# Constants, first loads and the first norm in one stage, and the rotary tables moved into the cross attention's dense stage

## The reference

```python
# first block
x = x + parallel_mixer(rms_norm(x, g_mix), w_in, conv_w, ..., w_out)       # 1024 -> 3088 columns, then mLSTM and gMLP
x = x + memory_cross_attention(rms_norm(x, g_xattn), rms_norm(mem, g_mem), w_q_x, w_kv_x, w_o_x)
x = x + hier_moe(rms_norm(x, g_moe), ...)
x = rms_norm(x, g_final)
# second block, two layers
for l in range(2):
    mix = token_mixer(x, positions, ...)       # four branches; one of them (_mla) rotates by positions
    x = layernorm(alpha * x + mix, ...)
    x = layernorm(alpha * x + hier_moe2(x, ...), ...)

def rms_norm(x, g):
    return x * rsqrt(mean(x * x, axis=-1) + 1e-6) * g

def _rope(x, positions):                       # half = 16
    inv = 10000.0 ** (-arange(half) / half)
    ang = positions[..., None] * inv
    cos, sin = cos(ang), sin(ang)
    ...
```

## Time and profile before

| | |
|---|---|
| median of 3 runs | 3036.12 us (3034.94 to 3040.34) |
| the profiled execution, whole | 3035.32 us |
| its span, first to last instruction | 3033.6 us |
| TensorE busy | 2463.5 us, 81% of the span |
| VectorE, ScalarE, GpSimd busy | 1301.4, 889.5, 407.8 us |
| mean granted TensorE clock | 0.900 of full |

### The profile page before, as it was taken

One profiled execution on the slowest core, in us unless ns is written; L12 is line 12 of the kernel. 1 busy time (PEld: TensorE's weight loads), 2 busy tenths in 40 slices (PEclk: granted clock), 3 DMA queues, 4 the chain that ended last, 5 costly groups with the idle time before them and its releaser, 6 DMA issues. The chain is left out here.

```text
span 3033.6 us, 50648 instructions
## 1 busy us (share of the span) xinstructions
PE 2463.5 (81%) x18120; PEld 1934.1 (64%) x18121; DVE 1301.4 (43%) x2776; ACT 889.5 (29%) x1677; POOL 407.8 (13%) x718
## 2 busy tenths in 40 slices
PE   4975799888888886869899869983959989869882
PEld 4963788854444446757677857763848667757661
DVE  4437345521111115634753544335644754453334
ACT  2233234211111113144532313322233633213221
POOL 1000000022122210000000134442000000024333
PEclk9988899889999998979999869996979999969996
DMA  3200242679999954022121479993212212459993
GB/s 127 85 1 1 70 139 58 278 319 403 411 410 404 395 219 152 29 70 61 44 62 52 155 291 345 381 363 137 70 35 70 61 51 63 164 197 374 383 388 140
DMA packets 209305, 565.80 MB, mean 187 GB/s; under 512 B 26598, under 2 KB 170598, under 8 KB 184592
## 3 DMA queue, kind: packets, MB, share of 16 engines
q1 hardware_dynamic: 191104, 538.73, 47.8%
q0 software_dynamic: 18064, 25.23, 2.5%
HBM read 560.46 MB, written 36.18 MB: 197 GB/s over the span
## 5 line engine op out<-in xcount | busy, mean ns | idle before, releaser
L1027 PE MATMUL ps<-m_gate_up,e_xT 128*64 128x256 f32 x1088 | 271.4, 413 | 64.1 <-DMA m_gate_up<-in_w_gate_up 57.9
L1027 PEld LDWEIGHTS ps<-r_gate_up,e_xT 128*64 128x64 f32 x2272 | 264.3, 143 | 91.3 <-issue 87.7
L1027 PE MATMUL ps<-r_gate_up,e_xT 128*64 128x128 f32 x2272 | 276.8, 283 | 41.4 <-DMA r_gate_up<-in_w_exp_gate_up 34.2
L1029 PE MATMUL ps<-r_gate_up,e_xT 128*64 128x128 f32 x2272 | 276.9, 283 | 0.0
L1027 PEld LDWEIGHTS ps<-m_gate_up,e_xT 128*64 128x64 f32 x1088 | 160.6, 150 | 177.0 <-issue 113.3
L1181 DVE TENSOR_TENSOR e_hid<-e_silu,ps 64x128 f32<-64x128 f32 (+1 forms) x210 | 70.2, 335 | 473.3 <-ACT e_silu L1069 469.3
L1029 PE MATMUL ps<-m_gate_up,e_xT 128*64 128x256 f32 x1088 | 271.5, 413 | 0.0
L1029 PEld LDWEIGHTS ps<-r_gate_up,e_xT 128*64 128x64 f32 x2272 | 264.3, 143 | 0.0
L1069 ACT ACTIVATE e_silu<-ps 64x128 f32<-64x128 f32 (+1 forms) x210 | 63.6, 303 | 654.7 <-PE ps L1029 654.7
L2195 PE MATMUL ps<-t_hT,t0a_t0g_w 128*128 128x512 f32 x768 | 199.4, 411 | 4.6 <-DVE t0a_t0g_w L2217 2.4
L2195 PE MATMUL ps<-t_hT,t1a_t1g_w 128*128 128x512 f32 x768 | 198.1, 409 | 4.6 <-DVE t1a_t1g_w L2217 2.4
(11 more groups left out here) (647 smaller groups left out, 4793.9 us busy)
## 6 DMA issues: line engine op xcount, KB each, us to landing
m_gate_up<-in_w_gate_up SPq DMA_DIRECT2D x32, 4096.0 KB, 39.0
r_gate_up<-in_w_exp_gate_up SPq DMA_DIRECT2D x64, 2048.0 KB, 31.1
m_down<-in_w_down SPq DMA_DIRECT2D x32, 2048.0 KB, 38.9
r_down<-in_w_exp_down SPq DMA_DIRECT2D x64, 1024.0 KB, 34.0
t0a_t0g_raw<-in_w_in SPq DMA_DIRECT2D x32, 512.0 KB, 3.8
t1a_t1g_raw<-in_w_in SPq DMA_DIRECT2D x32, 512.0 KB, 3.8
mixw_raw<-in_w_in SPq DMA_DIRECT2D x10, 1024.0 KB, 5.2
xaw_raw<-in_w_kv_x SPq DMA_DIRECT2D x8, 1024.0 KB, 5.4
```

The lines of the kernel that those rows point to most:

```text
L1027: nc.tensor.matmul(ps_gu[q][0:SLOTS], xT[:, c, :], ring.gu[s][:, 0, c, span], start=c == 0, stop=c == DC - 1)
L1029: last = nc.tensor.matmul(ps_gu[q][SLOTS:P], xT[:, c, :], ring.gu[s][:, 1, c, span], start=c == 0, stop=c == DC - 1)
```

## The change

The constants, the load, the gate columns, `mask_ge` and the first norm become one stage, `start_up`. Its four engine blocks run side by side:

- SyncE issues x in four transfers, one for each tile, each with its own semaphore, then the columns, then nine transfers in a list, of which four are small rows, one the positions and four the mixer's constants. It waits for the list at the end.
- GpSimd makes all constants, `mask_ge` with them.
- VectorE computes, for each tile as it lands, statistics with `bn_stats` and `bn_aggr`, and from them mean square plus epsilon; the factor of a tile (`reciprocal`) comes behind the statistics of the next one. At the end it makes the gate columns.
- ScalarE takes a root of a value set to one before anything else, then for each tile the root and the scaling of the tile into the mixer's `y`.

The rotary tables become a class `Rope`. The angle chain runs on VectorE as the `side` of the cross attention's `dense` after chunk 0, and the two sines run on ScalarE, by a new argument `act_side`, after its items of chunk 1. `dense` gets two more arguments, `pe_side` and `banks`, which no call in the program sets.

```diff
-def dense(nc, name, k, chunks, items, raw_ring=3, side=None, before=None):
+def dense(nc, name, k, chunks, items, raw_ring=3, side=None, before=None, act_side=None, pe_side=None, banks=8):
...
                             act.wait_ge(bank_full, i + 1)
-                            it.out(nc.scalar, ps[0:it.rows, i % 8, 0:it.n]).then_inc(emptied["act"], 1)
+                            it.out(nc.scalar, ps[0:it.rows, i % banks, 0:it.n]).then_inc(emptied["act"], 1)
+                    if act_side is not None:
+                        act_side(act, c)
...
+def make_constants(nc, k, pool, made):
...
+    for n in ("ident", "mask_le", "mask_lt", "mask_ge"):
+        g.memset(k[n][:], 0.0)
...
+    g.affine_select(k["mask_ge"][:], k["mask_ge"][:], [[1, n]], ALU.is_ge, -BIG, P - S, -1)
...
+def start_up(nc, k, x, rows_of_x, h, columns, column_rows, loads, col):
...
+            @block.sync
+            def _(sp):
+                for t in range(TT):
+                    sp.dma_start(x[:, t, :], rows_of_x[t * P:(t + 1) * P]).then_inc(x_landed[t], 16)
+                sp.dma_start(columns[:], column_rows).then_inc(columns_landed, 16)
+                for dst, src in loads:
+                    sp.dma_start(dst, src).then_inc(late_landed, 16)
+                sp.wait_ge(late_landed, 16 * len(loads))
+
+            @block.gpsimd
+            def _(pool):
+                make_constants(nc, k, pool, made)
+
+            @block.vector
+            def _(dve):
+                link = Chain(dve, chain)
+                vec.memset(r[:, 4, :], 1.0).then_inc(cleared, 1)
+
+                def squares(t):
+                    at = slice(t, t + 1)
+                    dve.wait_ge(x_landed[t], 16)
+                    for q in range(D // 256):
+                        last = vec.bn_stats(stats[:, t, q, :], x[:, t, q * 256:(q + 1) * 256])
+                    link(last)
+                    link(vec.bn_aggr(mv[:, t, :], stats[:, t]))
+                    link(vec.scalar_tensor_tensor(r[:, 3, at], mv[:, t, 0:1], mv[:, t, 0:1], mv[:, t, 1:2], ALU.mult, ALU.add))
+                    vec.tensor_scalar(r[:, 0, at], r[:, 3, at], 1e-6, None, ALU.add).then_inc(mean_ready, 1)
+
+                def factor(t):
+                    dve.wait_ge(root_ready, t + 1)
+                    vec.reciprocal(r[:, 2, t:t + 1], r[:, 1, t:t + 1]).then_inc(factors_ready, 1)
+
+                for t in range(TT):
+                    squares(t)
+                    if t:
+                        factor(t - 1)
+                factor(TT - 1)
+                dve.wait_ge(columns_landed, 16)
+                for l in range(2):
+                    for n, w, f in (("half_b_gate", 32, 0.5), ("minus_b_gate", DC, -1.0)):
+                        vec.tensor_scalar(k[n][:, l * w:(l + 1) * w], col(f"b_gate{l}")[:, 0:w], f, None, ALU.mult)
+
+            @block.scalar
+            def _(act):
+                act.wait_ge(cleared, 1)
+                sca.activation(r[:, 4, 0:1], r[:, 4, 1:2], ACT.Sqrt)
+                for t in range(TT):
+                    act.wait_ge(mean_ready, t + 1)
+                    sca.activation(r[:, 1, t:t + 1], r[:, 0, t:t + 1], ACT.Sqrt).then_inc(root_ready, 1)
+                    act.wait_ge(factors_ready, t + 1)
+                    sca.activation(h[:, t, :], x[:, t, :], ACT.Identity, scale=r[:, 2, t:t + 1])
...
-            rms_rows(nc, "mixn", [(lambda t: x[:, t, :], lambda t: y[:, t, :], TT, D)], 1e-6, k["mixer_loads"])
+            k["start_up"](y)
...
-            dense(nc, "xaw", k, chunks, items,
+            rope = Rope(nc, sb, k)
+            dense(nc, "xaw", k, chunks, items, side=lambda dve, c, emptied: rope.angles(dve) if c == 0 else None,
+                  act_side=lambda act, c: rope.sines(act) if c == 1 else None,
                   before=TurnSplit(nc, k, TT, lambda t, c: h[:, t, c * P:(c + 1) * P], hT, DC, col("g_xattn")))
...
+    def sines(self, act):
+
+        act.wait_ge(self.ready, 1)
+        self.nc.scalar.activation(self.k["cs"][:, 0], self.ang[:, 3], ACT.Sin)
+        self.nc.scalar.activation(self.k["cs"][:, 1], self.ang[:, 0], ACT.Sin)
...
-            load(nc, "ld", [(x[:], i["x"][0].rearrange("(t p) d -> p t d", p=P)), (columns[:], i["columns"])]
-                 + [(k["rows"][n], row(n)) for n in k["rows"]])
...
-            rope_tables(nc, k, i["positions"], cs)
...
+                loads = [(k["rows"][n], row(n)) for n in k["rows"]] + [
+                    (k["positions"][:], i["positions"]), (w_sT[:], i["w_sT"]), (g_head[:], row("g_head")),
+                    (ln_v[:, 0], row("ln_v_g")), (ln_v[:, 1], row("ln_v_b"))]
+                k["start_up"] = lambda h: start_up(nc, k, x, i["x"][0], h, columns, i["columns"], loads, col)
```

More of the change, by code:

```diff
@@ L141, in _ @@
                 for i, it in enumerate(items):
-                    if i >= 8:
-                        pe.wait_ge(emptied[items[i - 8].engine], nth[i - 8])
+                    if i >= banks:
+                        pe.wait_ge(emptied[items[i - banks].engine], nth[i - banks])
                     pairs = it.operands(w[:, it.chunk % 2])
@@ L152, in _ @@
                                 pe.wait_ge(first_low_ready, q // step + 1)
-                        last = nc.tensor.matmul(ps[0:it.rows, i % 8, 0:it.n], stationary, moving,
+                        last = nc.tensor.matmul(ps[0:it.rows, i % banks, 0:it.n], stationary, moving,
                                                 start=j == 0, stop=j == len(pairs) - 1)
                     last.then_inc(bank_full, 1)
+                    if pe_side is not None:
+                        pe_side(pe, i)
             @block.scalar
@@ L210, in _ @@
                             dve.wait_ge(bank_full, i + 1)
-                            it.out(nc.vector, ps[0:it.rows, i % 8, 0:it.n]).then_inc(emptied["dve"], 1)
+                            it.out(nc.vector, ps[0:it.rows, i % banks, 0:it.n]).then_inc(emptied["dve"], 1)
                     if side is not None:
@@ new lines, in start_up @@
+def start_up(nc, k, x, rows_of_x, h, columns, column_rows, loads, col):
+    vec, sca = nc.vector, nc.scalar
+    with Stage(nc, "up") as st:
+        stats = st.sb("stats", [P, TT, D // 256, vec.BN_STATS_DIM])
+        mv = st.sb("mv", [P, TT, vec.BN_AGGR_DIM])
+        r = st.sb("r", [P, 5, TT])
+        x_landed = [st.sem(f"x_landed{t}") for t in range(TT)]
+        columns_landed, late_landed, made, chain, cleared, mean_ready, root_ready, factors_ready = (
+            st.sem(n) for n in ("columns_landed", "late_landed", "const_made", "dve_chain", "cleared", "mean_ready",
+                                "root_ready", "factors_ready"))
+        with nc.Block() as block:
+            @block.sync
[43 more added lines that the diff above has]
+                    sca.activation(h[:, t, :], x[:, t, :], ACT.Identity, scale=r[:, 2, t:t + 1])
@@ L1272 @@
                                                                 ("ln2_g", 1024), ("ln2_b", 1024))])
-def load(nc, name, pairs):
-    with Stage(nc, name) as st:
-        landed = st.sem("landed")
-        with nc.Block() as block:
-            @block.sync
-            def _(sp):
-                for dst, src in pairs:
-                    sp.dma_start(dst, src).then_inc(landed, 16)
-                sp.wait_ge(landed, 16 * len(pairs))
 def running_log_sigmoid(nc, name, k, f, nf, after_from, b):
```

120 lines of the change are left out of this document (44 added, 76 removed).

## The result

| | before | after |
|---|---|---|
| median of 4 runs each | 3035.53 us (3032.71 to 3040.34) | 3003.78 us (2998.78 to 3004.67) |
| ratio after to before | | 0.989, interval [0.9873, 0.9908] |
| the profiled execution, its span | 3035.32 us, span 3033.6 us | 3003.62 us, span 3001.9 us |
| mean granted TensorE clock | 0.900 | 0.906 |

What follows compares the result with a forecast made beforehand. TensorE's idle first 37 us, a row of small stages, were taken as the stretch to cut: 35.79 - 15.5 = 20.3 us saved, tables 0. 3035.3 - 20.3 = 3015.0, with 0.8 for the median 3015.8 us; range 3011 to 3021.

Steps and rivals of the forecast that it cites:

- Loads: New first stage: first issue at 0.8, x's first tile landing at 4.2, SyncE's wait ending at 13.4 to 15.5 us.
- VectorE and ScalarE: New first stage: VectorE's statistics set the pace, ScalarE's last scaling ends at 15.3 us; 15.5 taken for the stage.
- GpSimd beside VectorE: New first stage: GpSimd's work until 8.7 us was taken not to slow VectorE; at an earlier row's price, end at 18.4.
- Rival 1: First stage ends late, at 17 to 25 us, by GpSimd dragging VectorE or slower transfers; 3018 to 3025 us; chance 0.13.
- First transpose: TensorE's start after the first stage: at 16.6 us, first matmul with weights 6.6 to 7.1 us later.
- The tables: Rotary tables moved into the cross attention's dense stage: hidden, slack 4.3 us left, sum 0.
- by more than 3 us in sum: Stages after the first: the prediction is wrong if their length changes by more than 3 us in sum.
- rival 4: Later stages: TensorE's clock takes the gain back, 3036 us or slower; otherwise shifts up to 3 us; chance 0.02.
- Rival 2: More saved, 22 us or more, by earlier loads, paired tiny instructions or better clock later; 3013 to 3010 us; chance 0.05.

Runs made afterwards that it cites:

- startup_only: Kernel before with the changed start, rotary tables in a stage of their own behind it; 3018.0 us over six runs (the 26.04 row adds a 4 us pause).
- before_all: Kernel before with idle instructions on all five engines (TensorE 242, VectorE 9, ScalarE 115, SyncE 113, GpSimd 99); started 31 us late, 4.1 us shorter behind the start.
- before_pe_dve: Kernel before with 242 idle instructions on TensorE and 9 on VectorE in its constants' stage; started 31 us late, 8.6 us shorter behind the start.

## Why the prediction was wrong

The steps of the start held.

- *Loads.* The first issue came at 0.80, the first tile was there at 4.43 (4.2 forecast), the last load at 14.9, inside 13.4 to 15.5.
- *VectorE and ScalarE.* The chain ended at 15.99 (15.3 forecast, 15.5 taken for the stage). The 0.7 us is the scaling, 1.15 us with gaps in place of 1.1, the first tile 0.2 us later, and one tiny instruction beside GpSimd.
- *GpSimd beside VectorE.* Four BN_STATS took 1.41 us beside it and 1.38 alone, so the price of the earlier trace rows did not apply, which agrees with the rule of the Trainium skill that was weighed ("SBUF — State Buffer", Who interferes with whom). Rival 1 did not happen. (Its 18.4 adds the 2.9 us lost to the 15.5 taken for the stage; from the chain's own 15.3 it is 18.2.)
- *First transpose* at 16.77 for 16.6; first matmul 6.8 us later (6.6 to 7.1). The start saved 20.2 of 20.3 us. Some of that closeness is luck: the stage's work ended 0.5 us later than the 15.5 taken, and the change to the next stage took 0.78 us (15.99 to 16.77) where 1.13 was carried over.
- *The tables* at nothing: right, with 4.8 us of slack where 4.3 was worked out.

The step that failed is that the stages after the first would change "by more than 3 us in sum" only if the prediction was wrong: rival 4's "small shifts of both signs are what I expect, up to 3 us in sum". They changed by 11.6 us net in the two traces and by 11.7 and 11.8 in the medians of two sets. The prediction took everything behind 36.92 to move by what the new stage saves, and a change of the first stage to act on later ones only through the time at which they start. The runs show one more way, which the diff does not show: how many instructions TensorE has ahead of a stage decides whether a refill meets its first weights, worth 1 to 3 us at t1. The rest of the 11.6 us, the larger part, is not traced to a cause; VectorE's count and where the buffers lie are candidates. Rival 2 had the sign and a mechanism close by (the granted clock stands better) with a chance of 0.05 and "a few us".

What is shown and what is not:

- *Shown:* the refill of TensorE's stream among t1's first weights, put in by 14 instructions in the changed kernel and taken out by 242 in the kernel before (with 9 on VectorE), costs 1.0 to 1.5 us at that place, and all twenty traces agree; in the kernel before, the longer idle time is followed by one more stretch at the low clock, and the stage is 2.8 us longer.
- *Supported, not shown:* with TensorE's count as in the kernel before and the others close to it, the changed code is as long behind the start as the kernel before, within 2.2 us by a median between two groups of runs, and three engines of the five play no measurable part. From the other side 4 to 9 of the 11.7 us, give or take 4, were reached without any of the changed code.
- *Spoken against:* the time of the start alone (-11.1 at 25.70 for the changed kernel, +2.0 at 26.04 for startup_only, though on two chips); either half of the change alone (-0.5; -0.4 and -5.3).
- *Open:* how the sum divides between VectorE's count, the buffers' addresses (350 against 386 GB/s), a late start, the chip and the experts of the last layer, and why before_all gained less than before_pe_dve. The stretches behind t0's and t1's output have one of two lengths, some 4.6 us apart, in repeats of one kernel too, so a single pair of traces can't divide it.

## What to carry to other kernels

Work out the stage that a change shortens as was done here; it held to 0.2 us, with two errors of 0.5 and 0.35 us against each other. Then widen the range on the side of gains and losses alike by what moves in the rest of the program without being edited: here 12 us of 3000, of which 1 to 3 us are traced to a dozen instructions fewer ahead of one weight load. To tell such a thing from the change's own merit, run the changed kernel with idle instructions that restore the old counts, check in the trace that the packet stands where it stood, run the changed kernel itself in every set, and place the idle instructions where the engine is idle: 119 of them on VectorE delayed this start by 8 us, 240 on TensorE by 31 us.

## What the hardware showed that was not expected

- Instruction streams are brought in during the run through DMA queues of their own, 16384 B at a time on q8 (87 packets) and 8192 B on q14 (50). With one q8 packet among them three weight transfers landed after 8.8 to 9.0 us instead of 7.5 to 7.8.
- The same load ran at 350 or 386 GB/s with no difference in its own instructions: 386 in all twelve traces with the moved tables, whose 16-byte buffer shifts the addresses, 350 in the other eight. The cause was not isolated.
- An instruction that only increments a semaphore is not free: 119 of them held VectorE from 0.93 to 12.34 us, 96 ns each; 240 on TensorE moved the next stage's first transfer from 7.17 to 38.05 us, 0.13 to 0.16 us each.
- A tiny SCALAR_TENSOR_TENSOR on one column took 0.62 us at 6.17 beside GpSimd's selects and 0.22 us at 8.62 without them, while BN_STATS were untouched. Like the slow TENSOR_TENSOR of the earlier trace rows it reads two tensors, BN_STATS one.
- The kernel before, unchanged, ran from 3021.9 to 3046.3 us in 86 runs of five sets; a single run tells little of a difference below some 10 us.
